# Two blocks of a hybrid transformer on one core: turn buffers of their own for the second rotary pair, a home of its own for the merged operand, windows loaded in two parts, and stacks first in ScalarE's slot of an attention

## What is computed

```
block one, twice:
  h = h + 0.5 * rmsnorm(swiglu(rmsnorm(h)))            # v = 0, 3
  u = rmsnorm(h);  proj = u @ w_in                     # mixer, v = 1, 4
  A = neighbourhood_attention(qa, ka, va, rpb)         # 8 x 16 windows of a grid 64 wide
  B = sliding_window_attention(rope(qb), rope(kb), vb, sink)
  C = differential_attention(rope(qc), rope(kc), vc, lam)
  merged = sum(sigmoid(gl) * (branch_i @ w_branch_i))  # i = A, B, C
  h = h + rmsnorm(merged @ w_out)
  h = h + 0.5 * rmsnorm(swiglu(rmsnorm(h)))            # v = 2, 5
block two, once:
  mixer of S (sliding window with sinks), F (forgetting attention) and LRU   # v = 6
  h = h + merged @ w_out;  h = h + swiglu(rmsnorm(h)); rmsnorm(h)            # v = 7
```

## Time and profile before

| | |
|---|---|
| median of 3 runs | 3554.92 us (3553.59 to 3557.11) |
| the profiled execution | 3558.35 us |
| its span | 3556.5 us |
| TensorE busy | 3459.4 us, 97% |
| VectorE, ScalarE, POOL busy | 50%, 39%, 10% |
| granted clock of TensorE, mean | 0.991 |
| DMA | 332.23 MB, 93 GB/s |
| chain of work that ended last | PE 91%, DVE 3%, ACT 3%, DMA 2% |

### The profile page before, as it was taken

How to read it: one execution, slowest core, us unless ns; L and a number is a source line. 1 busy time by engine, 2 the same in 40 slices (tenths; PEclk the granted TensorE clock), 3 DMA queues, 4 the chain that set the end, 5 groups by cost and what they waited for, 6 DMA issues and landing times.

```text
span 3556.5 us, 42770 instructions
## 1 busy us (share of the span) xinstructions
PE 3459.4 (97%) x17080; PEld 2877.5 (81%) x17080; DVE 1787.5 (50%) x3164; ACT 1373.2 (39%) x2437; POOL 346.7 (10%) x327
## 2 busy tenths in 40 slices
PE   8999999999999999999999999999999989999998
PEld 7888887878888888888887877888888878878887
DVE  5442565746544335432666655544248665544432
ACT  4222453634432233222454544432237363333221
POOL 0110110121011001100111021011000001201100
PEclk9999999999999999999999999999999999999999
DMA  3223332253232322233433253232322322323232
GB/s 137 95 92 98 103 101 78 69 137 95 72 107 95 93 92 91 95 95 94 109 83 86 73 142 95 78 101 95 92 89 87 90 61 66 107 83 101 95 94 73
DMA packets 110871, 332.23 MB, mean 93 GB/s; under 512 B 18248, under 2 KB 19016, under 8 KB 110672
## 3 DMA queue, kind: packets, MB, share of 16 engines
q1 hardware_dynamic: 98352, 306.82, 28.2%
q0 software_dynamic: 12320, 22.66, 3.1%
HBM read 306.23 MB, written 4.21 MB: 87 GB/s over the span
## 4 chain that ended last, share of the span: by engine, by line
PE 91%; DVE 3%; ACT 3%; DMA 2%; issue 1%; SPq 0%; POOL 0%; DVEq 0%; ACTq 0%
PE PS L702 90%; PE PS L1027 1%; ACT wh L1146 1%; DMA raw<-in_win 1%; DVE wl L1621 1%; DMA stk<-stk 0%; ACT tmp L1146 0%; ACT stk L1146 0%; DMA raw<-in_gu 0%; DVE stk L1903 0%; DMA tmp<-tmp 0%; DVE tmp L1931 0%; DVE small L1937 0%; DVE ul L2040 0%; DVE tmp L1952 0%
## 5 line engine op out<-in xcount | busy, mean ns | idle before, releaser
L702 PE MATMUL PS<-uh,wh 128*128 128x512 f32 (+1 forms) x3336 | 1267.6, 380 | 32.2 <-DVE ul L1649 15.1
L702 PE MATMUL PS<-uh,wl 128*128 128x512 f32 (+1 forms) x3336 | 1262.5, 378 | 0.0
L702 PE MATMUL PS<-ul,wh 128*128 128x512 f32 (+1 forms) x3336 | 1256.2, 377 | 0.0
L1621 DVE TENSOR_TENSOR wl<-raw,wh 128x1024 fp32r<-128x1024 f32 (+2 forms) x595 | 709.6, 1194 | 895.7 <-ACT wh L1146 893.4
L1146 ACT ACTIVATE wh<-raw 128x1024 fp32r<-128x1024 f32 (+2 forms) x595 | 584.0, 984 | 547.4 <-PE PS L702 534.0
L702 PEld LDWEIGHTS PS<-uh,wh 128*128 128x128 f32 x3336 | 630.6, 189 | 160.6 <-DVE tmp L2035 10.3
L702 PEld LDWEIGHTS PS<-ul,wh 128*128 128x128 f32 x3336 | 631.0, 189 | 120.4
L702 PEld LDWEIGHTS PS<-uh,wl 128*128 128x128 f32 x3336 | 629.8, 189 | 116.9 <-issue 1.4
L702 PE MATMUL PS<-gh,wh 128*128 128x512 f32 (+1 forms) x968 | 363.6, 376 | 0.0
L702 PE MATMUL PS<-gh,wl 128*128 128x512 f32 (+1 forms) x968 | 362.1, 374 | 0.0
L702 PE MATMUL PS<-gl,wh 128*128 128x512 f32 (+1 forms) x968 | 359.6, 372 | 0.0
(11 more groups left out here) (215 smaller groups left out, 3273.5 us busy)
## 6 DMA issues: line engine op xcount, KB each, us to landing
raw<-in_gu SPq DMA_DIRECT2D x220, 512.0 KB, 3.4
raw<-in_win SPq DMA_DIRECT2D x139, 512.0 KB, 3.5
raw<-in_dn SPq DMA_DIRECT2D x80, 512.0 KB, 3.5
raw<-in_wbr SPq DMA_DIRECT2D x72, 256.0 KB, 2.6
raw<-in_dn SPq DMA_DIRECT2D x40, 384.0 KB, 3.1
raw<-in_wout SPq DMA_DIRECT2D x24, 512.0 KB, 3.5
raw<-in_wv SPq DMA_DIRECT2D x20, 512.0 KB, 3.4
stk<-stk SPq DMA_DIRECT2D x72, 128.0 KB, 2.4
```

What stands on the lines that cost most here:

```text
L702: return e.matmul(out, lhs, rhs, start=start, stop=stop, skip_group_check=True)
L1621: tt(wl[:, p % 4, 0:n], raw[:, p % 3, 0:n], wh[:, p % 4, 0:n], SUB).then_inc(*S.lo.up(("lo", p)))
```

## The change

It has four parts.

1. **Rotary.** There are four turn buffers, each with a semaphore: q of C's second pair uses `rb` row 1, k of the first `tmp` row 2, k of the second `gates` row 0, all others `tmp` row 5. VectorE ropes q1 and k1 ahead of the stacks of q and k.
2. **The merged operand.** It has halves `mh`, `ml` of its own in the area that `stk` and `V` leave after attention A. ScalarE and VectorE make half m - 2 behind branch m, and 6 and 7 in `out`. The normed result goes to `y_u`; out's jobs use banks 3, 4, 5, 0, 1 and, for the split ones, (2, 0), (1, 5), (3, 4). In v = 6 the residual, its norm's low half and its sum follow each out job.
3. **ScalarE's slot.** It begins with the stacks; in F with `ahead` as well. `turned` comes next where the slot has no filler (and in F), and last otherwise, as before. In C a projection is stacked three slots after its end rather than two, on ScalarE and VectorE.
4. **Windows.** The four windows for query blocks 1 and 2 are read after merge step 0, the others after step 3 as before, with a semaphore each.

```diff
@@ -384,9 +384,9 @@
             if v < 6 and m > 4:
-                add(("out", v, m), "wout", (l, m), 8, [(2 * m + 1) % 6, (2 * m + 2) % 6], H2)
+                add(("out", v, m), "wout", (l, m), 8, [(2, 0), (1, 5), (3, 4)][m - 5], H2)
             else:
-                add(("out", v, m), "wout", (l, m), 8, [m % 6], C1)
+                add(("out", v, m), "wout", (l, m), 8, [(m + 3) % 6 if v < 6 else m % 6], C1)
     return jobs, pieces, fills
...
@@ -400,7 +400,7 @@
         self.n = len(units)
-        self.wait = 5 if name == "B" else 2
+        self.wait = {"B": 5, "C": 3}.get(name, 2)
...
@@ -462,7 +462,8 @@
         stk = sb("stk", [P, 12, TW], F32R, X)
-        y_x = sb("y_x", [P, 8, TW], F32, X)
+        mh = sb("mh", [P, 8, TW], F32R, X)
+        ml = sb("ml", [P, 8, TW], F32R, X + 8 * TW * 4)
         lru = sb("lru", [P, 20, 532], F32, X)
...
@@ -563,7 +564,7 @@
             i = 2 * j + r - 2
-            return V[:, i, :] if i < 5 else PT[:, i - 5, :]
+            return V[:, i + 1, :] if i < 4 else [PT[:, 1, :], PT[:, 2, :], V[:, 0, :], PT[:, 0, :]][i - 4]
...
@@ -583,7 +584,10 @@
-            return 2 if tag[0] == "k" and tag[2:] in (("C", 0), ("C", 1)) else 5
+            return {("q", "C", 1): 2, ("k", "C", 0): 1, ("k", "C", 1): 3}.get((tag[0], *tag[2:]), 0)
+
+        def turn_at(i):
+            return [tmp[:, 5, :], tmp[:, 2, :], rb[:, 1, :], gates[:, 0, :]][i]
...
@@ -888,7 +892,7 @@
                         w1, w2 = wh[:, p % 4, P * k:P * k + P], wl[:, p % 4, P * k:P * k + P]
-                        i = three(bank(job.banks[0]), w1, w2, uh[:, k, X0:TW], ul[:, k, X0:TW], k == 0, k == 7)
+                        i = three(bank(job.banks[0]), w1, w2, mh[:, k, X0:TW], ml[:, k, X0:TW], k == 0, k == 7)
                         if k == 7:
...
@@ -1272,30 +1276,29 @@
             def out(v):
-                last = 0 if v < 6 else 2
-                cols = slice(X0, TW)
-                E.wait_ge(S.mm, "job", ("g", v, last, 7), len(JOBS["g", v, last, 7].chunks) - 1)
-                for k in range(KT):
-                    for c in range(len(JOBS["out", v, 0].chunks)):
-                        E.wait_ge(S.pl, "macc", v, last, k, c)
-                    act(uh[:, k, cols], macc[:, k, cols], ACT.Copy).then_inc(*S.aa.up(("mh", v, k)))
+                for k in (6, 7):
+                    merged(v, k)
                 for m in range(KT if v == 6 else 5):
...
                         square("post", v, m, bank(job.banks[0]), 0.5)
-                        act(y_x[:, m, X0:TW], bank(job.banks[0]), ACT.Identity, scale=pcol(*POST[v], m)).then_inc(
+                        act(y_u[:, m, X0:TW], bank(job.banks[0]), ACT.Identity, scale=pcol(*POST[v], m)).then_inc(
                             *S.aa.up(("y", v, m, 0)))
+                    elif m:
+                        residual(m - 1)
                 if v < 6:
...
                 ahead(reach(JOBS["gate", 7, 0]))
-                E.wait_ge(S.mm, "job", ("out", v, 7), 0)
-                for m in range(KT):
-                    E.wait_ge(S.dn, "wr", v, m, 0)
-                    prepare(7, m)
-                    square("pre", 7, m, h[:, m, X0:TW])
+                residual(7)
+
+            def residual(m):
+
+                E.wait_ge(S.dn, "wr", 6, m, 0)
+                prepare(7, m)
+                square("pre", 7, m, h[:, m, X0:TW])
...
@@ -1427,8 +1430,15 @@
                 for n in range(A.n + A.lag + 4):
-                    if st == "F" and 0 <= n - A.lag < A.n:
-                        turned(v, st, n - A.lag)
+                    u = n - A.lag
+                    idle = n >= len(fill.quota) or fill.quota[n] == 0
+                    for job in fill.ended(n - A.wait):
+                        if job.kind in "qk":
+                            stack(job.tag)
+                    if st == "F":
+                        ahead(fill_reach(fill, n))
+                    if 0 <= u < A.n and (idle or st == "F"):
+                        turned(v, st, u)
                     if n < A.n:
...
@@ -1439,11 +1449,7 @@
                             tanh(*job.tag[1:])
-                    for job in fill.ended(n - A.wait):
-                        if job.kind in "qk":
-                            stack(job.tag)
-                    u = n - A.lag
-                    if st != "F" and 0 <= u < A.n:
+                    if 0 <= u < A.n and not (idle or st == "F"):
                         turned(v, st, u)
...
@@ -1453,11 +1459,23 @@
+            def merged(v, k):
+
+                last = 0 if v < 6 else 2
+                if v < 6:
+                    E.wait_ge(S.pv, "A", v, 31)
+                else:
+                    E.wait_ge(S.dv, "ob", v, 2, 3)
+                E.wait_ge(S.pl, "macc", v, last, k, 0)
+                act(mh[:, k, X0:TW], macc[:, k, X0:TW], ACT.Copy).then_inc(*S.aa.up(("mh", v, k)))
+
             def merge(v, n, m):
...
                 ahead(reach(JOBS["br", v, n, m]))
+                if n == (0 if v < 6 else 2) and m > 1:
+                    merged(v, m - 2)
...
@@ -1854,15 +1871,15 @@
                             *S.dn.up(("wr", v, m, c)))
+                    if m:
+                        low(7, m - 1)
+                        gather("pre", 7, m - 1)
                 if v < 6:
...
                 ahead(reach(JOBS["gate", 7, 0]))
-                for m in range(KT):
-                    low(7, m)
-                    if m < 7:
-                        gather("pre", 7, m)
+                low(7, 7)
...
@@ -1878,13 +1895,13 @@
                 E.wait_ge(S.mm, "job", tag, 0)
-                for dst, table in ((temp_of(tag), cos), (turn, sin)):
-                    if dst == turn and turn in turned:
-                        E.wait_ge(S.rp[turn == 2], "roped", turned[turn])
+                for dst, table in ((tmp[:, temp_of(tag), xs], cos), (turn_at(turn)[:, xs], sin)):
+                    if table is sin and turn in turned:
+                        E.wait_ge(S.rp[turn], "roped", turned[turn])
                     if which == "q":
-                        i = stt(tmp[:, dst, xs], ps, 0.125, table[:, :], MUL, MUL)
+                        i = stt(dst, ps, 0.125, table[:, :], MUL, MUL)
                     else:
-                        i = tt(tmp[:, dst, xs], ps, table[:, :], MUL)
+                        i = tt(dst, ps, table[:, :], MUL)
                 i.then_inc(*S.dv.up(("ev", tag, 0)))
...
@@ -2037,17 +2054,16 @@
                 E.wait_ge(S.aa, "mh", v, k)
-                tt(ul[:, k, X0:TW], macc[:, k, X0:TW], uh[:, k, X0:TW], SUB).then_inc(*S.dv.up(("m", v, k)))
+                tt(ml[:, k, X0:TW], macc[:, k, X0:TW], mh[:, k, X0:TW], SUB).then_inc(*S.dv.up(("m", v, k)))
...
                 ahead(reach(JOBS["br", v, n, m]))
-                if m == 7 and n == (2 if v == 6 else 0):
-                    for k in range(5):
-                        low_m(v, k)
                 gated(JOBS["br", v, n, m])
+                if n == (0 if v < 6 else 2) and m > 1:
+                    low_m(v, m - 2)
...
@@ -2057,13 +2073,13 @@
                 evacuate(JOBS["g", v, 2, 0], v)
+                rope(JOBS[q1], v)
                 ahead(reach(JOBS[q1]))
+                rope(JOBS[k1], v)
                 ahead(reach(JOBS[k1]))
                 stack(q)
-                rope(JOBS[q1], v)
                 stack(k)
                 ahead(reach(JOBS["v", v, "C", 0]))
-                rope(JOBS[k1], v)
                 ahead(reach(JOBS["v", v, "C", 1]))
...
@@ -2346,8 +2362,8 @@
                 for a, o in ((32, 0), (0, 32), (96, 64), (64, 96)):
-                    e.dma_start(tmp[o:o + 32, temp_of(tag), X0:TW], tmp[a:a + 32, turn_of(tag), X0:TW], accum_op=ADD).then_inc(
-                        *S.rp[turn_of(tag) == 2].land(("roped", tag)))
+                    e.dma_start(tmp[o:o + 32, temp_of(tag), X0:TW], turn_at(turn_of(tag))[a:a + 32, X0:TW], accum_op=ADD).then_inc(
+                        *S.rp[turn_of(tag)].land(("roped", tag)))
...
@@ -2370,14 +2386,15 @@
-            def windows_in(v):
+            def windows_in(v, part):
                 E.wait_ge(S.vw, "values", v)
-                E.wait_ge(S.pl, "macc", v, 1, 3, 0)
-                for j in range(1, 5):
+                if part:
+                    E.wait_ge(S.pl, "macc", v, 1, 3, 0)
+                for j in (2 * part + 1, 2 * part + 2):
                     for r in range(2):
                         src = bass.AP(VAL.tensor, (256 * r + window(j)[1]) * 512, [[64 * 512, 4], [512, 32], [1, 512]])
-                        e.dma_start(window_values(j, r), src).then_inc(*S.vi.land(("windows", v)))
+                        e.dma_start(window_values(j, r), src).then_inc(*S.vi[part].land(("windows", v)))
...
@@ -2398,8 +2415,8 @@
                     merge(v, 1, m, 2)
-                    if m == 3:
-                        windows_in(v)
+                    if m in (0, 3):
+                        windows_in(v, m // 3)
                 for x in range(2, 8):
```

19 lines of the change are left out of this document (9 added, 10 removed).

## The result

The changed kernel takes 3502.14 us (median of 4 runs, 3498.69 to 3503.76), the kernel before in the same session 3556.02 (3553.59 to 3557.30): a ratio of 0.9848, 95% interval 0.9831 to 0.9865, 53.9 us less. The forecast was 3506, from 49.8.

A forecast was written before the change was run, and what follows sets the result against it. The prediction took TensorE's work, busy 3459.4 of 3556.5 us, to bound the kernel. Its terms, 16 + 13.5 + 9 + 5.3 + 6 + 1 - 1 = 49.8 us below 3555.8, gave 3506, range 3493 to 3528.

The forecast's parts named there:

- What bounds it: Whole kernel: TensorE's work bounds it; only its 97 us of idle time and losses to a lowered clock can return.
- Rotary, 16: Start of attention C, twice: separate turn buffers end TensorE's waits and the slow clock; gain 16 us, bounds 12.5 and 17.7.
- Merged operand, 13.5: Start of out, twice: halves made between merges and free banks end TensorE's wait; gain 13.5 us, bounds 9.5 and 14.7.
- Windows, 9: Attention A, twice: windows in two parts and stacks ahead of an exponential end waits; gain 9 us, bounds 0 and 11.5.
- half the windows now go out three merge steps earlier, where nothing waits: Merges before attention A: half the windows are issued some 8 us earlier, at a place where nothing waits.
- v = 6, 5.3: Out and start of the last FFN: earlier halves and residuals per job shorten waits; gain 5.3 us, bounds 1.5 and 6.3.
- F, 6: Attention F: ScalarE's wh and stacks first end three TensorE waits for masked scores; gain 6 us, bounds -5 and 14.
- My sign for F: Attention F in the new profile: TensorE busy over 96 in a stretch of under 99.
- The rest, 0: Copies before the exponential where nothing fills, 1 us; B's early stacks, 0, bounds -2 and +2; C's later stacks, -1.
- the first (new waits): New waits take over: windows give 3, F 0, v = 6 gives 3; gain 35.5 us, 3520; chance 0.22.
- The second (the clock gives nothing back): Vanished stalls do not restore the clock, so 12.5 us of the gain stay lost: 3518.5; chance 0.08.
- The fourth, ScalarE blocked in order: Stacks at the head of 33 slots hold back exponentials; from 1.5 us each the gain is lost; 3575; chance 0.03.

The follow-up runs named there:

- experiments 10: The changed kernel with out's banks as before (0, 1, 2 for the first three jobs), halves still made between merges: 3507.17 us, ratio 0.9860 to the kernel before.
- experiment 11: The changed kernel with the merged operand's halves at their old places, but the new banks and home: 3508.89 us, ratio 0.9866 to the kernel before.
- experiment 5: The changed kernel with its windows in one part, as before: 3505.18 us, ratio 0.9861 to the kernel before.
- experiment 3: The kernel before with only the windows in two parts: 3558.60 us, ratio 1.0011 to the kernel before.
- Experiment 4: The kernel before with only ScalarE's new order and C's stacks one slot later: 3539.72 us, ratio 0.9960 to the kernel before.
- experiment 7: The changed kernel with attention B's stacks at the end of ScalarE's slot again: 3503.79 us, ratio 0.9857 to the kernel before.
- experiment 8: The changed kernel with F's stacks back at the end of the slot, weights' high halves still first: 3509.38 us, ratio 0.9875 to the kernel before.
- experiment 1: The kernel before with the rotary part alone: 3542.46 us, ratio 0.9963 to the kernel before.
- experiment 2: The kernel before with the merged operand's part alone, including v = 6's residuals per job: 3535.20 us, ratio 0.9953 to the kernel before.

## Why the prediction was right, and where not

The sum, 49.8, came near 53.9 partly by luck, as its misses cancelled: by stages F gave 11.6 more than its term, while the windows gave 3 less and B and the end of C lost 5.6 that the sum did not have.

- *What bounds it*: right. No stage gained anything but idle time, slow clock and, 3.5 us in all, the longer matmuls at the waits, which the prediction leaves out.
- *Rotary, 16*: 17.0 (9.0 + 8.0), and 17.1 at its place when alone, though the whole time then fell by 12.3 only. Right in mechanism and size, within its bounds.
- *Merged operand, 13.5*: 14.1 (4.9 + 2.9 and 4.8 + 1.5). Right. I hadn't said how much each of its halves would be worth; experiments 10 and 11 show that neither alone does it.
- *Windows, 9*: attention A won 6.0, of which the split is worth some 3 beside the rest (experiment 5) and nothing alone (experiment 3). The step that failed is "half the windows now go out three merge steps earlier, where nothing waits". The weight loads of those merges wait: they land in 10.9 us instead of 3.4, and the changed kernel has ScalarE idle for `raw` for up to 5.08 us there. Experiment 4, which holds the other half of the same step, the stack ahead of the exponential, shows 5.7 in A, with the copies' 1.1 and a slow stretch in it; how much of it is the stack stays open. By the sharing rule of the Trainium skill ("DMA: Bandwidth & Descriptors") I had priced the term at 3: that was nearer for the split.
- *v = 6, 5.3*: 5.6 (1.7 + 3.9), with 0.83 left of the 3.22.
- *F, 6*: 17.6. This is the term that was mis-sized most, and it lies above its own bound of 14. I had bounded it by TensorE's idle time in one stretch of F, and left out the slow clock there, although the first part of the prediction says that a stall costs twice, and the longer matmuls at the waits: over the whole of F idle time gave 11.5, the clock 3.3 and those matmuls 2.8. My sign for F, TensorE busy "over 96 in a stretch of under 99", can't hold in us, as that stretch has only 90.09 busy; as a share it came: the same instructions now take 89.5 us with 86.4 busy. And I had counted only the three waits that name VectorE's scores. The others, for banks that VectorE empties (`macc`, `tmp`) and for `obl`, hung on the same late VectorE, since it works in order; both `wh` and the stacks were behind it, with 10.0 and 6.5.
- *The rest, 0*: B lost 2.4 in two layers, just beyond its bound of -2: 0.8 net for the stacks by experiment 7, the rest slow matmuls behind the longer wait in v = 4. The end of C lost 3.2, all slow clock, which no term had. C's later stacks cost nothing; no wait for them shows. The copies at the ends of attentions gave 0.56 in each A (1.56 to 1.00) and nothing in B (1.85 to 1.95), as TensorE now waits there for VectorE's `tmp L1987`.

Of the rivals, the first (new waits) came true in part, in A for 3 us and in B for 2.4; its price for F was wrong. The second (the clock gives nothing back) is refuted where long stalls went: in none of the kernels with the rotary part, and in none with the merged part, are there slow matmuls at those places. What it said of small stalls holds, see below. The fourth, ScalarE blocked in order, has one place in each layer (B, 0.9 us), far from 33 places at 1.5. The range and the chances I would leave as they were.

## What to carry to other kernels

Price a stall by what its stage takes against the same matmuls elsewhere, not by idle time alone: slow clock came with the idle time in most stages here (2.6 us with 6.26, 2.9 with 4.75), though not in all (none with 1.54 in v = 6), and the matmuls at a wait are longer too. Where an engine works in order and idles before late work, look at what stands behind it that could have run: moving `wh` and the stacks to the head of F's slot, with no instruction added or removed, was the largest single gain. And moving a transfer to an earlier place buys only what the loads of that place can spare.

## What else the runs showed of the hardware

**The same small stalls slow the clock in one run and not in the next.** At the end of C in v = 1 TensorE idles 0.74, 0.35 and 1.18 us in every kernel. In the changed one the clock is halved twice: some sixteen short matmuls take 0.42 us instead of 0.28 between the second and the third wait, and 8 matmuls take 0.63 behind the third. In experiment 8, with the same instructions there, none do. This is its stretch at the same time as the changed kernel's above, with 38 matmuls instead of 28 and a clock of 1.00 instead of 0.78:

```profile
543.00:549.00 6.00, 4.83 (x38) 4.46 (x38) 0.18 (x1) 2.62 (x5) 0.00 (x0) 1.00 0.14 44
```

Of the fourteen profiles ten have slow matmuls there in v = 1, five of them twice, and five have them once in v = 4, for about 1.6 us each time. The work at that place is the same in all, so it is not the work that decides; that it is only a matter of when the stall falls fits, but no run here shows it by itself. With several such places it may make up for much of the 5 to 9 us by which runs of one kernel differ: of experiment 1's runs those of 3545.5 and 3545.9 have a mean granted clock of 0.992, those of 3536.9 and 3537.5 one of 0.994. The Trainium skill ("TensorE: Matmul & The Clock Gate", "What's actually happening") has the gate's windows run free of the kernel, and this agrees.

**VectorE stands still while POOL adds.** In the changed kernel a `wl` that starts beside an addition of POOL's takes 2.33 us instead of 1.23 (VectorE's and POOL's timelines):

```profile
882.93 2.33 DVE L1639 TENSOR_TENSOR wl<-raw,wh 128x1024 fp32r<-128x1024 f32 x1
```

```profile
882.49 1.68 POOL L2375 TENSOR_TENSOR macc<-macc,tmp 128x512 f32<-128x512 f32 x1 [6.68 <-DVE tmp L2052]
```

The `wl` that take over 1.5 us grew from 8 to 21, because the halves between merges bring `wl` and addition together: they are 21 in experiment 2 as well, and 9 in experiment 11, which has the halves at their old places. All `wl` together took 709.6 us and take 725.6, and no wait of TensorE shows for it. When this `wl` began, the addition had 882.49 + 1.68 - 882.93 = 1.24 us to go, and `wl` was longer by 1.10. The Trainium skill ("SBUF — State Buffer", "Who interferes with whom") says that a VectorE operation with both inputs in SBUF contends with a GpSimd instruction that reads SBUF, and calls the shared ports an exclusive lock; the trace agrees.
